# Gated linear attention: another order of ACT's and VectorE's work around the states

## The reference, cut to what matters

```
b = cumsum(log_a) within a chunk
q_e = q * exp(b);  k_e = k * exp(-b);  k_d = k * exp(b_last - b)
scores = mask(q_e @ k_e^T);  kv = k_d^T @ v
state_n = exp(b_last) * state_{n-1} + kv_n
o = scores @ v + q_e @ state_in
```

## Time and profile before

| | |
|---|---|
| median of 3 runs | 1954.1 us |
| profiled execution, its own time | 1955.2 us |
| its span, first to last instruction | 1953.9 us |
| TensorE, VectorE, ACT, GpSimd busy | 97%, 50%, 35%, 20% |
| mean granted TensorE clock | 0.983 |
| load of a unit of `w_in`, issue to landing | 5.0 us |

### The profile page before, as it was taken

One profiled execution on the slowest core, in us unless ns is written; L12 is line 12 of the kernel. 1 busy time (PEld: TensorE's weight loads), 2 busy tenths in 40 slices (PEclk: granted clock), 3 DMA queues, 4 the chain that ended last, 5 costly groups with the idle time before them and its releaser, 6 DMA issues.

```text
span 1953.9 us, 21675 instructions
## 1 busy us (share of the span) xinstructions
PE 1887.1 (97%) x8817; PEld 1515.5 (78%) x8821; DVE 972.1 (50%) x1300; ACT 678.7 (35%) x907; POOL 382.9 (20%) x343
## 2 busy tenths in 40 slices
PE   7899999999999999999999999998899999999998
PEld 5787888888867457888888878776687888888887
DVE  5695443433447764543434447555436544443432
ACT  5663221222224673322222334554322333222212
POOL 2004110110326584220101131111001231110103
PEclk9999999999999899999999999999999999999999
DMA  4222323232322202232323233111223223233221
GB/s 152 87 86 87 108 86 108 87 108 87 103 91 74 79 1 87 87 108 86 108 87 108 73 94 101 44 52 54 84 87 102 87 87 108 92 103 101 94 92 60
DMA packets 167170, 172.35 MB, mean 88 GB/s; under 512 B 7480, under 2 KB 164288, under 8 KB 167072
## 3 DMA queue, kind: packets, MB, share of 16 engines
q1 hardware_dynamic: 164544, 163.75, 25.9%
q0 software_dynamic: 2528, 7.22, 1.1%
HBM read 168.69 MB, written 2.14 MB: 87 GB/s over the span
## 4 chain that ended last, share of the span: by engine, by line
PE 83%; DVE 7%; ACT 6%; issue 3%; POOL 1%; DMA 0%; another core or an unknown queue 0%; SPq 0%; ACTq 0%; DVEq 0%
PE bank L760 26%; PE bank L761 26%; PE bank L762 26%; ACT whi L1138 2%; DVE wlo L1592 1%; PE bank L788 1%; DVE XC L1671 1%; POOL pt L683 1%; DVE t L1843 1%; PE bank L946 1%; PE bank L1040 1%; PE bank L925 1%; DVE work L1845 1%; ACT pt L1340 0%; PE bank L1035 0%
## 5 line engine op out<-in xcount | busy, mean ns | idle before, releaser
L760 PE MATMUL bank<-Ahi,whi 128*128 128x512 f32 (+1 forms) x1400 | 556.3, 397 | 25.3 <-DVE SR L1604 12.7
L761 PE MATMUL bank<-Alo,whi 128*128 128x512 f32 (+1 forms) x1400 | 550.7, 393 | 0.0
L762 PE MATMUL bank<-Ahi,wlo 128*128 128x512 f32 (+1 forms) x1400 | 550.1, 393 | 0.0
L1592 DVE TENSOR_TENSOR wlo<-stage,whi 128x2048 fp32r<-128x2048 f32 (+2 forms) x146 | 331.7, 2272 | 432.0 <-ACT whi L1138 432.0
L1138 ACT ACTIVATE whi<-stage 128x2048 fp32r<-128x2048 f32 (+2 forms) x152 | 287.3, 1890 | 460.4 <-PE bank L762 460.4
L760 PEld LDWEIGHTS bank<-Ahi,whi 128*128 128x128 f32 (+1 forms) x1400 | 265.8, 190 | 90.7 <-issue 27.1
L762 PEld LDWEIGHTS bank<-Ahi,wlo 128*128 128x128 f32 (+1 forms) x1400 | 265.8, 190 | 57.0
L761 PEld LDWEIGHTS bank<-Alo,whi 128*128 128x128 f32 (+1 forms) x1400 | 266.1, 190 | 56.5 <-issue 1.2
L762 PE MATMUL bank<-Hhi,wlo 128*128 128x512 f32 x688 | 267.6, 389 | 0.0
L760 PE MATMUL bank<-Hhi,whi 128*128 128x512 f32 x688 | 267.6, 389 | 0.0
L761 PE MATMUL bank<-Hlo,whi 128*128 128x512 f32 x688 | 267.6, 389 | 0.0
(11 more groups left out here) (333 smaller groups left out, 2155.3 us busy)
## 6 DMA issues: line engine op xcount, KB each, us to landing
stage<-in_mlp_w_up SPq DMA_DIRECT2D x32, 1024.0 KB, 5.3
stage<-in_mlp_w_down SPq DMA_DIRECT2D x32, 1024.0 KB, 5.0
stage<-in_w_in SPq DMA_DIRECT2D x22, 1024.0 KB, 5.0
stage<-in_w_ffn_in SPq DMA_DIRECT2D x22, 1024.0 KB, 4.9
stage<-in_w_ffn_out SPq DMA_DIRECT2D x8, 1024.0 KB, 5.2
stage<-in_rec_w_in SPq DMA_DIRECT2D x7, 1024.0 KB, 5.3
stage<-in_att_w_in SPq DMA_DIRECT2D x6, 1024.0 KB, 5.3
stage<-in_rec_w_out SPq DMA_DIRECT2D x4, 1024.0 KB, 4.9
```

The source lines that it names most:

```text
L760: e.matmul(ps, hi, rh, start=first, stop=False)
L761: e.matmul(ps, hi, rl, start=False, stop=False)
L762: return e.matmul(ps, lo, rh, start=False, stop=last)
L1592: e.tensor_tensor(lo_of(u)[:, 0:nk, 0:n], stage[s][:, 0:nk, 0:n], f32(hi_of(u)[:, 0:nk, 0:n]), ALU.subtract).then_inc(s_lo[s], 1)
```

## The change

Nothing is computed otherwise; instructions change their place within the programs of ACT and VectorE. On ACT the root and the scaling of a head's outputs come in the same pass of the loop, around the high half of the next weight and ahead of the copies of the values; `half_tanh` goes ahead of a high half. On VectorE the two read-outs of r are taken out of `silu_r` into `gate_r`, which goes ahead of the states, and `silu_r` goes between the two groups of states (head 0: both behind the states). The low half of the unit behind GA(h-1) (in head 0 of K1) goes behind a group of states, and `out_over_root` to the end of the pass, ahead of the low half of the next R unit.

```diff
--- before.py
+++ after.py
@@ -1478,8 +1478,6 @@
         hi(u_of["V", 1] + 1)
         copy_v(1)
         for h in range(4):
-            if h:
-                out_scaled(h - 1)
             copy_kdt(h)
             if h == 0:
                 hi(u_of["Q", 1] + 1)
@@ -1488,24 +1486,25 @@
             else:
                 hi(u_of["R", h] + 1)
                 out_hi(h - 1)
+                half_tanh(h)
                 hi(u_of["GA", h - 1] + 1)
-                half_tanh(h)
                 gate_tanh(h - 1)
             if h < 3:
                 decays(h + 1)
                 decay_factors(h + 1)
-            else:
-                hi(u_of["GA", 3] + 1)
             out_squares(h)
             if h < 3:
                 remaining(h + 1)
+            out_root(h)
             if h == 0:
                 hi(u_of["K", 1] + 1)
             elif h < 3:
                 hi(u_of["V", h + 1] + 1)
+            else:
+                hi(u_of["GA", 3] + 1)
+            out_scaled(h)
+            if 0 < h < 3:
                 copy_v(h + 1)
-            out_root(h)
-        out_scaled(3)
         gate_tanh(3)
         hi(u_of["GA", 3] + 2)
         out_hi(3)
@@ -1995,9 +1994,12 @@
                         op = e.scalar_tensor_tensor(ST[d][:, i, :], ST[d][:, i - 1, :], dec[:, d, n:n + 1], ps, ALU.mult, ALU.add)
                     op.then_inc(*(ring.take(label) if state_frees(i) else (s_st, 1)))
 
+        def gate_r(h):
+            for m in (2 * h, 2 * h + 1):
+                scale_out(SR[:, m, :], ("r", m))
+
         def silu_r(h):
             for m in (2 * h, 2 * h + 1):
-                scale_out(SR[:, m, :], ("r", m))
                 e.wait_ge(s_rth, m + 1)
                 e.scalar_tensor_tensor(SR[:, m, :], rth[m % 2][:, :], 1.0, SR[:, m, :], ALU.add, ALU.mult).then_inc(s_sr, 1)
 
@@ -2033,29 +2035,32 @@
         for c in range(8):
             e.scalar_tensor_tensor(X[:, c, :], X[:, c, :], c1("fin1", c), sqt[:, :], ALU.mult, ALU.mult).then_inc(s_x2, 1)
         for h in range(4):
-            if h:
-                out_over_root(h - 1)
             masked(h)
             if h == 0:
                 lo(u_of["Q", 1] + 1)
-                lo(u_of["R", 0] + 1)
                 scale_out(QK[:, 4, :], ("qk", 4))
                 scale_out(QK[:, 6, :], ("qk", 6))
             else:
                 lo(u_of["R", h] + 1)
                 gated(h - 1)
-                lo(u_of["GA", h - 1] + 1)
                 gated_lo(h - 1)
+                gate_r(h)
+            states(h, 0)
+            if h:
                 silu_r(h)
-            states(h, 0)
+            else:
+                lo(u_of["R", 0] + 1)
             states(h, 1)
             if h == 0:
+                gate_r(0)
                 silu_r(0)
             else:
+                lo(u_of["GA", h - 1] + 1)
                 gate_a(h - 1)
             if h < 3:
                 decays(h + 1)
                 queries(h + 1)
+            out_over_root(h)
             if h == 0:
                 lo(u_of["K", 1] + 1)
                 scale_out(QK[:, 5, :], ("qk", 5))
@@ -2064,7 +2069,6 @@
                 lo(u_of["V", h + 1] + 1)
             else:
                 lo(u_of["GA", 3] + 1)
-        out_over_root(3)
         gate_a(3)
         lo(u_of["GA", 3] + 2)
         gated(3)
```

## The result

The changed kernel takes 1924.34 us in the median of 4 runs (1923.40 to 1925.12), the kernel before 1953.78 (1953.26 to 1954.29, 4 runs): a ratio of 0.9849, 95% interval 0.9832 to 0.9866. The forecast was 1923.9. The profiled execution took 1923.4 us with a span of 1922.2.

What follows compares the result with a forecast made beforehand. TensorE, busy 97%, was taken to lose time to late bank read-outs and the lower clock behind them; 26.5 - 0.3 + 4.0 = 30.2 us saved, giving a median of 1923.9 us, 8-in-10 range 1921.5 to 1930.

Steps and rivals of the forecast that it cites:

- Part 1: Rows read out ahead of the low half on VectorE: gate product starts without a wait, saving 26.5 us.
- Part 2: Root and scaling ahead of the value copies on ACT: the waits of the transposes shrink, saving 4.0 us.
- z behind the low half of V(h+1): z's bank is freed behind this low half on VectorE; charged 0.15 us in heads 1 and 2, 0.3 in all.
- The R product after head 0: Its bank is freed by the masking behind the later low half; 0.1 us charged against 0.47 us saved.
- The transposes: TensorE's waits for ACT's write of On, 4.1 us in 3 waits, were to go; under 0.2 us left.
- The loads that are issued later: Weight loads issued some 3 or 16 us later; costed at nothing, at most 5 us of DMA wait a head.
- rival A: Waits go but the stage still falls to 1.2 GHz; 19.4 us saved, 1934.7 us; 6%.
- Paid twice: Waits of 3.03 and 4.24 us cost their length and lower clock behind; 10.8 us of clock counted as saved.
- The table: ACT's Sqrt table load: 1.28 us by the row, against about 2.66 by the skill, which would give 28.8 us saved.
- Rival C: Slower: a late root delays R's low half and the next head's R product; 1958 us with 11 us late; 3%.
- Rival B: New waits at z and the R products take part of the gain; 20.8 to 26 us saved, 1928 to 1933; 13%.
- D: No change: another releaser frees the bank TensorE waits for, so the wait keeps its length; 1954 us; 2%.

Runs made afterwards that it cites:

- e1: The kernel after with the new places of root, scaling and value copies taken back; 1927.63 us, ratio 0.9869.
- e4: The kernel before with r's two read-outs ahead of the low half of V(h+1) in heads 1 to 3, low half and silu still ahead of states; 1939.79 us.
- e3: The kernel before with only the low half of K1 moved behind the first group of states of head 0; 1947.52 us, ratio 0.9971.
- e5: The kernel after with four additions ahead of the read-outs of r in heads 1 to 3, a wait of 1.74 us in each; 1929.34 us.
- e2: The kernel before with only root, its reciprocal, scaling and value copies in their new places; 1948.41 us, ratio 0.9972.
- e6: The kernel after with seven additions ahead of the read-outs of r in heads 1 to 3, a wait of 3.92 us in each; 1941.67 us.
- e7: The kernel after with scaling and value copies on ACT ahead of the high half of the next R unit; 1932.79 us, ratio 0.9895.
- e9: The kernel after with five additions ahead of the read-outs of r in heads 1 to 3, a wait of 2.46 us in each; 1933.72 us.
- e11: The kernel after with ten additions ahead of the read-outs of r in heads 1 to 3, a wait of 6.10 us in each; 1949.39 us.
- e10: The kernel after with six additions ahead of the read-outs of r in heads 1 to 3, a wait of 3.19 us in each; 1936.51 us.

## Why the prediction was right

**The sum.** 30.2 us were forecast; the stage is 30.55 us shorter, and the medians are 29.4 us apart. That the median came out within 0.4 us of the forecast is in part luck: single executions of before, in all sessions, lie between 1948.18 and 1956.36 us. Part 1, 26.5 us: the stretches of 13.70 to 14.81 us became 7.71, 7.71, 7.70 and 7.70 against the 7.72 worked out of the earlier trace rows, and saved 26.55. Part 2, 4.0 us: e1, which lacks it, is 4.15 us longer in the stage than after. The upper bound was added up wrongly: with every new wait at nothing the prediction's terms give 26.5 + 4.1 = 30.6 us, not 31.0.

**Each wait that could come next.** z behind the low half of V(h+1): charged 0.15 us a head, measured 7.24 against 7.17 us, so 0.07. The R product after head 0: charged 0.1, measured 0.23, and its releaser is the masking, as worked out. The charge was low because it put this product 1.09 us behind the start of the transposes, their length; in the trace of before it starts 0.85 us behind (1254.53 - 1253.68), which would have given 0.34. The transposes: no wait of TensorE is left. The loads that are issued later: no wait for wlo in the stage. The states behind the read-outs end within the gate product (e4 shows what it costs where they don't, 1.8 and 2.2 us).

**The clock** (rival A, 6%). It came back: 1.00 in the stage of after. e3 isolates it in head 0, and e1 and e5 show it at 1.00 beside waits of up to 1.83 us. "Paid twice" fits head 0 alone (3.0 us behind 3.03); behind 4.24 it was 2.3 to 2.9. What the prediction didn't see is that the 10.8 us before were one draw. With the same waits e2 paid 8.6 and e3 paid 1.4 us where before's head 3 paid 2.9. The term was right because it was taken from the very rows to be removed; as an estimate for other waits it was too high, which is e6's miss (expected 7.8, measured 4.8).

**The table.** The prediction set the 2.66 us of the Trainium skill (ScalarE: Activation LUTs, "What ACT_TABLE_LOAD costs") against the row. After, the load starts at 1288.52 and the root at 1289.81, the next instruction at 1290.02. A drain of 1.38 us is not there, though now the high half of a weight stands right behind. The row decides.

**Why the read-out was so late.** The prediction names the 2.29 us of the low half, and the earlier trace rows show VectorE idle for 7.67 us ahead of it. ACT in order, before, head 1:

```profile
1265.78 1.91 ACT L1138 ACTIVATE whi<-stage 128x2048 fp32r<-128x2048 f32 x1 [5.07 <-PE bank L762]
```

The high half of V(2) starts only when TensorE has ended R(1), which is when the 16 state products start. Behind it come the low half (2.29), O2l (1.29) and the read-out (0.68): 6.2 us together, of which the 16 products cover 2.1. So the whole chain stood ahead of the read-out, and not the low half alone.

**Rival C's price was wrong.** It counted R's margin as 2.3 us, that of the low half. The masking behind it leaves 1.4 us by the prediction's own figures (1309.9 - 1308.5), and e7 shows this bank as the one that TensorE waits for. Rival B's waits stayed within the 0.4 us charged, and D fell with the first line of the waits.

## What to carry to other kernels

In an engine that works strictly in order, find for each instruction when its result is wanted, not when its input is ready: a low half that nobody wanted for over 20 us, and whose input wasn't ready, stood ahead of a 0.7 us read-out that frees a bank, and TensorE waited 4.24 us each time. Then work through the next wait of every bank in the ring, with the clock times of the engine that reads it out. In heads 1 to 3 the read-outs' move alone gave 14.7 us (e4); with the low half and silu behind states too e1 gave 26.8, of which head 0 has 6.0. A wait of TensorE is worth its length, and a lower clock may come on top. In the stage that was nothing behind up to 2.56 us, 3.0 us behind the 3.03 of head 0, nothing or 1.7 us behind 3.19, and 1.4 to 2.9 us behind every wait of 3.9 us or more. Take that part from the rows of the wait itself, not from a neighbour, and as a range.

## What the runs showed of the hardware

The fall of the clock behind a wait is no fixed price. Of nine waits of 1.68 to 2.56 us put in (e5, e9, e7) none was followed by 1.2 GHz, of three of 3.19 us one, of three of 3.92 us all; and waits of 4.24 us cost between 1.4 and 2.9 us, as did those of 6.10. Where it falls it may do so within the wait (1322.2 against 1326.27 in e11) or after TensorE has started again (1318.7 against 1317.75 in e10). The price is about half of the time that TensorE works at 1.2 GHz: 6.2, 4.8, 5.6 and 6.0 us in the four heads of before, for 3.0, 2.3, 2.7 and 2.9 us. Two heads of one execution, with the same instructions and the same wait, came out 1.7 us apart.

Length alone doesn't decide it. The 3.03 us wait in head 0 cost 2.9 to 3.0 us in all three traces that have it (before, e2, e4), and 3.19 us in heads 1 to 3 cost nothing twice. At one place that no run changed, before the stage, a wait of 2.3 to 2.8 us was followed by 1.2 GHz in 3 of the 13 traces (before, e2, e5). In before (columns of the clock's row as in rows 2):

```profile
149.00 0.50 PE L760 MATMUL bank<-YSh,whi 128*128 128x512 f32 x1 [2.79 <-DVE wlo L1592]
```
```profile
151.00:152.00 1.00, 1.00 (x4) 0.81 (x3) 0.54 (x1) 0.00 (x0) 0.00 (x0) 0.50 0.99 337
```

In after:

```profile
149.71 0.50 PE L760 MATMUL bank<-YSh,whi 128*128 128x512 f32 x1 [2.80 <-DVE wlo L1591]
```
```profile
151.00:152.00 1.00, 1.00 (x6) 0.82 (x5) 0.44 (x1) 0.53 (x1) 0.00 (x0) 1.00 0.86 260
```

What makes the difference between the traces these runs don't show.
